# Linear attention: one dense group fewer between the chunks of the second and third head, two between the chunks of the last head

## What is computed

```python
att = jnp.einsum('bthd,bshd,btshd->btsh', qc, kc, jnp.exp(diff))      # causal inside the chunk
o = (jnp.einsum('btsh,bshv->bthv', att, vc)
     + jnp.einsum('bthd,bhdv->bthv', qc * jnp.exp(b), S))
S = (S * jnp.exp(b_last)[..., None]
     + jnp.einsum('bshd,bshv->bhdv', kc * jnp.exp(b_last[:, None] - b), vc))
# before the loop:  z = h @ w_in  (columns of gate_g and gate_d are used only after both branches)
```

## Time and profile before

| | |
|---|---|
| median of 3 runs | 1896.09 us (1893.98 to 1897.71) |
| the profiled execution | 1893.62 us, its span 1891.8 us |
| PE busy | 1859.4 us, 98% of the span |
| ACT busy | 716.5 us, 38% |
| DVE busy | 1153.3 us, 61% |
| POOL busy | 845.2 us, 45% |

### The profile page before, as it was taken

How to read it: one execution, slowest core, us unless ns; L and a number is a source line. 1 busy time by engine, 2 the same in 40 slices (tenths; PEclk the granted TensorE clock), 3 DMA queues, 4 the chain that set the end, 5 groups by cost and what they waited for, 6 DMA issues and landing times. The chain is left out here.

```text
span 1891.8 us, 33399 instructions
## 1 busy us (share of the span) xinstructions
PE 1859.4 (98%) x12841; PEld 1697.2 (90%) x12841; DVE 1153.3 (61%) x2313; ACT 716.5 (38%) x1309; POOL 845.2 (45%) x674
## 2 busy tenths in 40 slices
PE   6999999999999999999999999999999999999998
PEld 6689999998898888888789988999999999988887
DVE  5699999344555433566664523756666556466658
ACT  5433212223333356555553212443333333333335
POOL 3242222423322241111013220477888876799866
PEclk9999999999999999999999999999999999999999
DMA  5132332322212263354554341232233222465323
GB/s 177 29 104 82 117 112 80 102 80 80 80 62 76 74 188 134 116 207 175 202 199 139 113 158 49 95 130 84 90 112 124 95 84 85 173 240 179 135 67 125
DMA packets 167396, 224.77 MB, mean 119 GB/s; under 512 B 11272, under 2 KB 122670, under 8 KB 166478
## 3 DMA queue, kind: packets, MB, share of 16 engines
q1 hardware_dynamic: 161262, 203.88, 32.0%
q0 software_dynamic: 5984, 18.82, 2.9%
HBM read 152.87 MB, written 67.34 MB: 116 GB/s over the span
## 5 line engine op out<-in xcount | busy, mean ns | idle before, releaser
L1188 PE MATMUL ring<-n_hi,piece_hi 128*128 128x352 f32 (+1 forms) x1304 | 431.4, 331 | 0.7 <-DVE n_lo L2419 0.7
L1190 PE MATMUL ring<-n_hi,piece_lo 128*128 128x352 f32 (+1 forms) x1304 | 419.7, 322 | 0.0
L1189 PE MATMUL ring<-n_lo,piece_hi 128*128 128x352 f32 (+1 forms) x1304 | 418.7, 321 | 0.0
L3281 POOL TENSOR_TENSOR piece_lo<-piece_whole,piece_hi 128x1024 fp32r<-128x1024 f32 (+2 forms) x48 | 105.9, 2206 | 499.7 <-ACT piece_hi L1758 499.5
L1745 ACT ACTIVATE arena<-ring 128x352 f32<-128x352 f32 (+6 forms) x358 | 147.0, 435 | 383.5 <-PE ring L1190 283.4
L3451 POOL TENSOR_TENSOR weight_lo<-weight_raw,weight_hi 128x512 fp32r<-128x512 f32 x152 | 224.8, 1497 | 111.0 <-ACT weight_hi L2158 109.9
L1188 PEld LDWEIGHTS ring<-n_hi,piece_hi 128*128 128x128 f32 (+1 forms) x1304 | 244.4, 187 | 8.0 <-issue 4.8
L1189 PEld LDWEIGHTS ring<-n_lo,piece_hi 128*128 128x128 f32 (+1 forms) x1304 | 245.2, 188 | 0.4
L1190 PEld LDWEIGHTS ring<-n_hi,piece_lo 128*128 128x128 f32 (+1 forms) x1304 | 244.1, 187 | 0.3
L2505 DVE TENSOR_SCALAR_CACHE_REDUCE arena<-arena 128x384 uint8<-128x384 f32 (+6 forms) x224 | 190.5, 874 | 1.4 <-DVE arena L2505 0.2
L3478 POOL TENSOR_TENSOR down_lo<-down_raw,down_hi 128x512 fp32r<-128x512 f32 x79 | 129.7, 1672 | 39.5 <-ACT down_hi L2254 39.4
(11 more groups left out here) (408 smaller groups left out, 4778.0 us busy)
## 6 DMA issues: line engine op xcount, KB each, us to landing
piece_whole<-w_in SPq DMA_DIRECT2D x54, 512.0 KB, 3.7
projected_rows<-arena SPq DMA_DIRECT2D x44, 528.0 KB, 2.7
rows_raw<-ffn_rows SPq DMA_DIRECT2D x21, 768.0 KB, 5.2
arena<-projected_rows SPq DMA_DIRECT2D x12, 1056.0 KB, 6.3
weight_raw<-w_ffn_gate SPq DMA_DIRECT2D x11, 1024.0 KB, 5.5
weight_raw<-w_ffn_up SPq DMA_DIRECT2D x11, 1024.0 KB, 7.8
down_raw<-w_ffn_down SPq DMA_DIRECT2D x3, 3072.0 KB, 10.4
arena<-projected_rows SPq DMA_DIRECT2D x16, 528.0 KB, 3.6
```

The lines of the kernel that those rows point to most:

```text
L1188: pe.matmul(out, lhi, rhi, start=first, stop=False)
L1189: pe.matmul(out, lhi, rlo, start=False, stop=False)
L1190: return pe.matmul(out, llo, rhi, start=False, stop=last)
L3281: ins = g.tensor_tensor(lo, raw, hi, ALU.subtract)
```

## The change

`head_groups` gets a table. All 24 groups stay. Before: head 0, 1 and 2 have 4 groups before the chunks, one after chunk 2, one after chunk 5, one after the chunks; head 3 has 3 before. After: head 0 is unchanged; heads 1 and 2 have 4 before, one after chunk 4, one after the chunks; head 3 has 3 before, one after chunk 1 and one after chunk 3. In the last head `hi_piece(N_IN + 1)` moves from i = 1 to i = 4. SP's stores and loads follow the groups.

```diff
         def head_groups(h, part):
 
-            k = 7 * h
-            ks = {"before": range(k, k + (4 if h < GH - 1 else 3)), 2: [k + 4], 5: [k + 5], "after": [k + 6]}[part]
-            return [(GLA0 + k // 3, k % 3) for k in ks if k < 24]
+            parts = ((("before", 4), (2, 1), (5, 1), ("after", 1)), (("before", 4), (4, 1), ("after", 1)),
+                     (("before", 4), (4, 1), ("after", 1)), (("before", 3), (1, 1), (3, 1)))
+            k = sum(c for done_ in parts[:h] for _, c in done_)
+            for name, c in parts[h]:
+                if name == part:
+                    return [(GLA0 + j // 3, j % 3) for j in range(k, k + c)]
+                k += c
+            return []
...
-                    spill_groups(head_groups(h, 2) + head_groups(h, 5))
+                    spill_groups([k for i in range(NTP) for k in head_groups(h, i)])
...
                     spill_groups(head_groups(h, "before"))
+                    spill_groups([k for i in range(NTP) for k in head_groups(h, i)])
                     gate_row(0)
...
-                    if i in (2, 5):
-                        for k in head_groups(h, i):
-                            dense(*k)
+                    for k in head_groups(h, i):
+                        dense(*k)
...
-                    if i in (2, 5):
-                        for k in head_groups(h, i):
-                            staged(*k)
+                    for k in head_groups(h, i):
+                        staged(*k)
                     if h == GH - 1 and 3 <= i < 7:
                         od_upper(OD_ORDER[i - 3])
-                    if h == GH - 1 and i == 1:
+                    if h == GH - 1 and i == 4:
                         hi_piece(N_IN + 1)
```

More of the change, by code:

```diff
@@ L368, in build @@
                 plan("go", h, i), plan("ds", h, i)
-                if i in (2, 5):
-                    for k in head_groups(h, i):
-                        plan_d(*k)
+                for k in head_groups(h, i):
+                    plan_d(*k)
             plan("go", h, NTP)
```

## The result

The changed kernel took 1911.38 us (median of 6 runs, 1910.1 to 1916.63) where the kernel before took 1897.14 beside it: ratio 1.0084, 95% interval 1.0072 to 1.0096. It is 14.2 us slower; 10 were forecast, with 1910 as the upper end of the range. Its profiled execution took 1916.63 us with a span of 1914.8, so it is the slowest of the six, 5 us above their median.

What follows compares the result with a forecast made beforehand. TensorE was taken to bound heads 1 and 2, without idle time there, dense groups covering side work. 2 x (2.1 + 3.2) - 0.3 = +10.3 us on the profiled 1893.62, plus 2.5 to the median: 1906, range 1901 to 1910.

Steps and rivals of the forecast that it cites:

- The stalls: Heads 1 and 2: TensorE waits for side work that lost its group, 2.1 us at chunk 4, 3.2 at chunk 7.
- Chunk 4's part: Heads 1 and 2: ScalarE's copies come late behind the uncovered Sigmoid, so TensorE loses 2.1 us per head.
- chunk 7's: Heads 1 and 2: VectorE's mask is late behind uncovered gate rows, 1.9 us, plus 1.3 for GpSimd's hold, 3.2 per head.
- The hold by GpSimd: Heads 1 and 2, behind chunk 5: a GpSimd subtraction delays the first gate row by 1.3 us; rival of no hold 0.17.
- Head 3: Last head: groups behind chunks 1 and 3 remove waits of 1.05 us, late rounding costs 0.75, so 0.3 us is gained.
- the late rounding: Head 3: ScalarE's rounding moved to i = 4, with its subtraction, costs 0.75 us, within bounds of nothing and 1.8.
- The first wait: Start of head 3's chunks: TensorE's 1.14 us wait for a ScalarE copy behind the Sigmoid stays.
- The loads of `og_whole`: Last head: SP's six loads come some 10 us later but stay covered; too late, or the clock: 0.05 together.
- the term for TensorE's clock behind the new pauses: Heads 1 and 2: the forecast's sum holds no loss from a lower TensorE clock after the new waits.
- TensorE's clock falls in the new pauses: Rival, heads 1 to 3: half rate for two chunks each adds 8 us, 1914, with a group 1922; 0.05 with late loads.

Runs made afterwards that it cites:

- the pauses filled: Changed kernel plus unused matmuls in TensorE's waits at chunks 4 and 7 of heads 1 and 2: +7.0 us against before, ratio 1.0040.
- the gate rows covered: Changed kernel with both gate rows of heads 1 and 2 moved from behind chunk 5 to behind chunk 4: +5.3 us against before, ratio 1.0027.
- head 3 undone: Changed kernel with head 3's two groups ahead of its chunks again and the rounding back behind chunk 1: +18.4 us against before, ratio 1.0089.
- covered kernel: Changed kernel with Sigmoid, chain start and gate rows of heads 1 and 2 moved under dense groups: +2.9 us against before, ratio 1.0006.
- the long pause filled: Changed kernel with 20 unused matmuls in chunk 7's wait of heads 1 and 2, chunk 4's waits left empty: +9.8 us against before, ratio 1.0053.

## Why the prediction was wrong

- **The stalls** were right, in place and size. Forecast: 2.1 + 3.2 us per head, less 0.3 in head 3, 10.3 in all. With the pauses filled, heads 1 to 3 take 148.79 us against 138.33 before: 10.46. Chunk 4's part is 2.15 and 1.93 us (the heads with the gate rows covered, against 47.67 and 47.82), chunk 7's 3.05 and 3.13.
- **The hold by GpSimd** was right: gate rows of 3.92 us beside the subtraction and 2.67 away from it; waits of 3.29 and 1.98 us with and without it in the kernel before. The rule of the Trainium skill ("SBUF — State Buffer", "Who interferes with whom") agrees with both. The prediction missed a gate row that goes first, in head 3 of the kernel before; it kept its 1.32 us, and the subtraction took 1.44 us where others of its size take 1.27 to 1.31:

```profile
939.44 1.32 DVE L2799 SCALAR_TENSOR_TENSOR arena<-arena 128x1056 f32<-128x1056 f32 x1
940.44 1.44 POOL L3281 TENSOR_TENSOR piece_lo<-piece_whole,piece_hi 128x512 fp32r<-128x512 f32 x1 [21.51 <-ACT piece_hi L1758]
```

- **Head 3** was off by half a us: +0.2 and not -0.3. The group behind chunk 3 does not cover the second gate row, because it waits for that row's mask itself (0.63 us), and the late rounding's subtraction holds an `od_lower` (2.12 us, 1.26 for the others), which turned the wait of 0.33 us into 1.00, near the 0.75 us that the prediction allowed for the late rounding. The first wait, which was to stay, is 0.3 us shorter.
- **The loads of `og_whole`**, now issued at 973.74, led to no wait of over 0.2 us.
- **The step that failed** is the term for TensorE's clock behind the new pauses, which the sum puts at nothing. As the rival "TensorE's clock falls in the new pauses" it stood with its price, 1914 to 1922, and got part of 0.05, since "the 1.14 us wait changed nothing" and no row of the stage showed a fall. One short wait in one execution was taken as evidence for waits of 1.2 and 3.3 us. What the runs show: heads with all three pauses open fell to 0.91 to 0.97 in six of six (three profiles of two heads), with the pauses filled in none of two, with the side work covered in none of four. The Trainium skill's warning ("TensorE: Matmul & The Clock Gate", "Why this matters for your kernels"), cited beside that rival, was the right one to weigh. The falls here were less regular than a rule would have them: one head fell behind 0.7 and 1.2 us, and another did not behind 3.33.
- **Its price** was of the right order: a head lost 1.5 to 4.8 us to the clock where the rival had 4 for two chunks and 8 with a group. The error was the chance. Over all runs the mean granted clock was 0.9947 with the pauses open (16 runs, head 3 undone among them) and 0.9978 before (52 runs): 0.0031 x 1911 / 0.5 = 12 us more at the lower level, and half of that, 6 us, lost if TensorE works all that time, an upper estimate. The covered kernel gave 3.5 to 5. With the stalls that is 14 to 16 us, against +14.2, +16.7 and +18.4 measured.

What stays open: the profiles differ by 5.7 us behind head 3 (935.2 to 940.9 us from there to the end). Nearly all of it is TensorE's waits of over 0.3 us there, 0.8 to 5.0 us in all: for GpSimd's `piece_lo` about 74 and 97 us behind head 3, for its `weight_lo` at 267, for VectorE's `x_low` at 732. Without them the lengths are 934.2 to 935.3 us, and 936.6 in one whose clock fell there. The four kernels with unused matmuls are the four shortest (waits of 0.8 to 2.1 us; the others 1.8 to 5.0), and why is open. So the gain by filling the pauses is not all the clock's. The 3.0 and 8.6 us within the heads of the two profiles are, and the 3.5 to 5 us by which the covered kernel gained more than its stalls agree with them.

## What to carry to other kernels

When a group of matmuls is moved away from a place, ask first which slow work of the other engines ran under it, and move that work along: with the three pieces under the remaining groups the same move cost nothing that could be measured. A pause of TensorE in dense work is to be priced twice, once as the wait and once for the clock behind it, about 1.5 to 5 us for each head here with pauses of 3.3 us and less; the absence of a fall behind a shorter wait does not exclude it. Unused matmuls in such a wait are a quick test of which part is the clock's, if it is read in the windows of the stage itself: the time of the whole kernel also changed for another reason.

## What was not expected of the hardware

- The fall of the clock differs from run to run at these pauses: 3.3 us of pause at chunk 7 and 0.6 + 1.2 us in chunk 4 gave 0.91 in one profile and 0.97 in the next; a lone 3.29 us gave no fall, nor did 0.63 and 3.33 us in one head of two, and 0.7 and 1.2 us in chunk 4 with the long pause filled gave one in one head of two.
- The clock also falls where TensorE works without a pause. In eight of the thirteen profiles of this study it is 0.98 from 690 to 765 us, as in the first one of the changed kernel. In these head 1 begins at 818.75 to 819.37 us, in four of the others at 816.19 to 816.85; in the fifth the clock had fallen at 330 us instead, and it begins at 819.35. That this makes the spread of the kernel before, 1893 to 1901 us, is not shown: among its 52 runs time and mean clock hardly go together. The row of the changed kernel:

```profile
690.00:765.00 75.00, 75.00 (x520) 64.06 (x520) 25.10 (x55) 42.11 (x63) 18.79 (x22) 0.98 0.45 151
```

- A dense group can be held up by its own bank, as the one behind chunk 3 of head 3 was for 0.63 us: a group covers only what is late after it has started.
